# The chunk state kept in PSUM: the evacuating engines write it back, instead of identity matmuls on TensorE

## The reference

```
def step(S, inp):
    r_t, w_t, k_t, v_t, kk_t, kka_t = inp
    sa = jnp.einsum('bhvk,bhk->bhv', S, kk_t)
    S = (S * w_t[:, :, None, :]
         - sa[..., None] * kka_t[:, :, None, :]
         + v_t[..., None] * k_t[:, :, None, :])
    y_t = jnp.einsum('bhvk,bhk->bhv', S, r_t)
    return S, y_t
```

## Time and profile before

| what | us |
|---|---|
| median of 3 runs | 2519.12 (2517.28 to 2519.45) |
| the profiled execution | 2521.04 |
| its span in the trace | 2519.3 |
| TensorE busy | 2282.6 (91%) |
| VectorE busy | 1435.9 (57%) |
| ScalarE busy | 1062.2 (42%) |
| one turn of the recurrence in steady state | 38.67 |

### The profile page before, as it was taken

One profiled execution on the slowest core, in us unless ns is written; L12 is line 12 of the kernel. 1 busy time (PEld: TensorE's weight loads), 2 busy tenths in 40 slices (PEclk: granted clock), 3 DMA queues, 4 the chain that ended last, 5 costly groups with the idle time before them and its releaser, 6 DMA issues.

```text
span 2519.3 us, 43613 instructions
## 1 busy us (share of the span) xinstructions
PE 2282.6 (91%) x16514; PEld 1690.7 (67%) x16514; DVE 1435.9 (57%) x2446; ACT 1062.2 (42%) x2072; POOL 282.8 (11%) x249
## 2 busy tenths in 40 slices
PE   3789999899999999979899999988789998999998
PEld 1566776566666666658688888856666585787876
DVE  6777888344454454444555455558974565434445
ACT  3455666245455455532322222332167623323233
POOL 2101000112122121210000000019600000000000
PEclk6899999799999999969999999999999998999998
DMA  2234456313212223023233333312221031333332
GB/s 95 79 118 130 158 163 176 83 36 69 65 40 65 56 54 65 19 77 98 76 90 94 97 95 96 96 59 67 67 76 34 26 92 54 97 94 90 100 90 77
DMA packets 387985, 208.37 MB, mean 83 GB/s; under 512 B 81520, under 2 KB 370696, under 8 KB 387592
## 3 DMA queue, kind: packets, MB, share of 16 engines
q1 hardware_dynamic: 387216, 206.21, 28.9%
q10 hardware_dynamic: 632, 0.21, 0.0%
HBM read 176.96 MB, written 29.43 MB: 82 GB/s over the span
## 4 chain that ended last, share of the span: by engine, by line
PE 61%; DVE 21%; ACT 10%; issue 6%; DMA 1%; SPq 1%; DVEq 0%; POOL 0%; ACTq 0%; POOLq 0%
PE bank L1465 13%; PE bank L1467 12%; PE bank L1466 12%; PE bank L517 3%; DVE w_lo L1620 3%; DVE dconv L1873 3%; PE bank L500 2%; PE bank L482 2%; ACT w_hi L1231 2%; PE bank L539 1%; PE bank L458 1%; PE bank L504 1%; PE bank L443 1%; PE bank L432 1%; PE bank L483 1%
## 5 line engine op out<-in xcount | busy, mean ns | idle before, releaser
L1465 PE MATMUL bank<-xl,w_hi 128*128 128x512 f32 (+1 forms) x1568 | 632.7, 404 | 65.4 <-DVE xl L1625 40.0
L1466 PE MATMUL bank<-xl,w_lo 128*128 128x512 f32 (+1 forms) x1568 | 617.6, 394 | 0.0
L1467 PE MATMUL bank<-xl,w_hi 128*128 128x512 f32 (+1 forms) x1568 | 617.4, 394 | 0.0
L1231 ACT ACTIVATE w_hi<-w_raw 128x1024 fp32r<-128x1024 f32 (+2 forms) x282 | 284.7, 1010 | 421.5 <-PE bank L1467 416.8
L1620 DVE TENSOR_TENSOR w_lo<-w_raw,w_hi 128x1024 fp32r<-128x1024 f32 (+2 forms) x282 | 333.8, 1184 | 140.9 <-ACT w_hi L1231 129.4
L1465 PEld LDWEIGHTS bank<-xl,w_hi 128*128 128x128 f32 (+1 forms) x1568 | 296.6, 189 | 171.2 <-issue 48.0
L1467 PEld LDWEIGHTS bank<-xl,w_hi 128*128 128x128 f32 (+1 forms) x1568 | 297.1, 189 | 65.3 <-issue 1.8
L1466 PEld LDWEIGHTS bank<-xl,w_lo 128*128 128x128 f32 (+1 forms) x1568 | 297.6, 190 | 62.7 <-issue 4.0
L1465 PE MATMUL bank<-xh,w_hi 128*128 128x512 f32 x480 | 198.1, 413 | 51.1 <-DVE w_lo L1620 46.0
L1466 PE MATMUL bank<-xh,w_lo 128*128 128x512 f32 x480 | 192.9, 402 | 0.0
L1467 PE MATMUL bank<-xh,w_hi 128*128 128x512 f32 x480 | 192.7, 401 | 0.0
(11 more groups left out here) (321 smaller groups left out, 3645.9 us busy)
## 6 DMA issues: line engine op xcount, KB each, us to landing
w_raw<-in_a_w_in SPq DMA_DIRECT2D x64, 512.0 KB, 4.1
w_raw<-in_b_w_in SPq DMA_DIRECT2D x64, 512.0 KB, 4.0
w_raw<-in_w_ffn_up SPq DMA_DIRECT2D x44, 512.0 KB, 3.8
w_raw<-in_w_in SPq DMA_DIRECT2D x36, 512.0 KB, 3.7
w_raw<-in_a_w_out SPq DMA_DIRECT2D x16, 512.0 KB, 4.0
w_raw<-in_b_w_out SPq DMA_DIRECT2D x16, 512.0 KB, 4.0
w_raw<-in_w_ffn_down SPq DMA_DIRECT2D x16, 512.0 KB, 4.0
d_g<-sq SPq DMA_DIRECT2D x16, 256.0 KB, 2.1
```

What stands on the lines that cost most here:

```text
L1231: A(w_hi[0:rows, slot, 0:nkb, 0:ncol], w_raw[0:rows, slot, 0:nkb, 0:ncol], ACT.Copy).then_inc(s_hi, 1)
L1465: mm(outp, wh, xlo, start=start, stop=False)
L1466: mm(outp, wl, xhi, start=False, stop=False)
L1467: return mm(outp, wh, xhi, start=False, stop=stop)
```

## The change

The identity matmuls of line 449 go. In phase 2 the evacuating engine, after the copy to `sv`, executes the same operation a second time with bank 6 as its output: the scaled state stays in bank 6. The matmul of line 464 of the next chunk then adds to what stands there; for the first chunk of a tile, whose state is zero, it starts the sum. A new semaphore for each head tells TensorE that the write is done, and line 464 waits for it beside the wait for u.

```
@@ recurrence_tensor, phase 0
                     if c:
                         state_output(j, b, c)
-                    for h in range(2):
-                        mm(bank[6][rows[h], 0:C], ident[rows[h], rows[h]], sv[b][rows[h], c, h, :],
-                           start=True, stop=False)
@@ recurrence_tensor, phase 2
                         pe.wait_ge(R["u_copied"][h], NCH * j + c + 1)
+                        if c:
+                            pe.wait_ge(R["state_seeded"][h], (NCH - 1) * j + c)
                         last = mm(bank[6][rows[h], 0:C], bt[b][:, c, rows[h]], sv[b][:, c, h, :],
-                                  start=False, stop=True)
+                                  start=c == 0, stop=True, skip_group_check=True)
@@ recurrence_evac, phase 2
                 scaled(sv[b][hs, c + 1, h, :], bank[6][hs, 0:C], st_pc[j % 3][hs, c:c + 1]).then_inc(R["s_copied"][h], 1)
+                scaled(bank[6][hs, 0:C], bank[6][hs, 0:C], st_pc[j % 3][hs, c:c + 1]).then_inc(R["state_seeded"][h], 1)
```

More of the change, by code:

```diff
@@ L371, in program @@
             "centered_copied", "y_squared", "var_summed", "y_rstd_made", "y_finished", "bonus_weighted")}
-        for n in ("e_copied", "inverse_made", "state_zeroed", "tiles_loaded", "ends_loaded", "rhs_copied", "u_copied", "s_copied"):
+        for n in ("e_copied", "inverse_made", "state_zeroed", "tiles_loaded", "ends_loaded", "rhs_copied", "u_copied", "s_copied", "state_seeded"):
             R[n] = [sem(f"{n}{h}") for h in range(2)]
```

## The result

The changed kernel takes 2541.8 us (2539.8 to 2545.5, 4 runs) against 2519.3 before: 1.0086 times as long, 95% interval 1.0073 to 1.0099, 22.5 us more. The forecast of 2521.5 (2511.5 to 2530) was wrong, and its chance for "slower" was only 0.35.

The account below looks back on a forecast made before the run. TensorE was taken as the bound over most of a period; -0.36 + 0.05 + 0.20 + 0.21 + 0.05 = +0.15 us, times 15 = +2.3 us, carried to the median: 2521.5 us, range 2511.5 to 2530.

Parts of the forecast that it names:

- the sum of a period: One period of the recurrence, 38.67 us before: gains from removed matmuls and costs of added writes together +0.15 us.
- Most of the identity passes come out as nothing: Removing a chunk's two identity matmuls frees at most 0.12 us; counted as gain only at chunks 4, 6 and 7.
- steps 6 and 9: Chunks 2 and 3 of a period: TensorE waits there for VectorE anyhow, so the removed matmuls gain nothing.
- step 0: Chunk 0 of a period: the products wait until ScalarE has stored V, so the removed matmuls gain nothing.
- The near price: Cost of one added write behind an evacuation of the same partitions: 0.20 us on VectorE, 0.21 on ScalarE.
- Steps 8 and 9: VectorE's write ahead of four masks delays L787, for which TensorE waits already: +0.20 us a period.
- Step 14: ScalarE's write ahead of the weight-panel cast L655 delays the cast and TensorE's L443: +0.21 us a period.
- rival 3: Both engines swallow the writes; five chunks gain 0.12 us, less 0.10 at chunk 5: 7.5 us, 2511.6; chance 0.10.
- steps 3 and 15: Chunks 1 and 5: removed matmuls would gain, but VectorE's added writes delay TensorE's later starts: +0.05 us each.
- -0.36: Gain a period at chunks 4, 6 and 7, where TensorE's next operation starts without a wait: 3 x 0.12 us.
- The second wait costs nothing: L464's added wait on the previous chunk's write counted zero; as a rival, 0.09 us later per chunk, 2531; chance 0.07.
- the dear prices: Rival: added writes cost 0.31 us on VectorE and 0.35 on ScalarE, nothing overlapping: +9.4 us, 2528.5; chance 0.28.

## Why the prediction was wrong

The step that failed is the one by which the sum of a period was turned into time: "+0.15 us a period, times 15" took the clock as it was. The prediction had the full clock in the row of the period, named the clock only at its end as something that nothing counted, and gave it no rival and no chance. The change lengthened two waits of TensorE and took away the passes that had filled part of others. Its periods at full clock account for 1.5 of the 22.5 us; the other 21 came from the clock that this cost: 51 us at 1.2 GHz in the profiled execution.

Point by point:

- *Most of the identity passes come out as nothing*: right. The waits at steps 6 and 9 grew by the 0.12 us that each pair had filled, and at step 0 a wait of 0.35 us opened where there had been none. (The changed kernel with filler in its waits has that one too, and the full clock, so it is not enough by itself.) That this was not free was the mistake: a pass that costs no time because TensorE would wait anyhow still keeps it busy. I had written these off as "nothing".
- *The near price*, 0.20 and 0.21: right. The next operation of the same first partition starts 0.20 behind on VectorE (620.61 to 620.81) and 0.22 on ScalarE (630.91 to 631.13). PSUM as the destination costs VectorE nothing more than SBUF (275 ns both). ScalarE is faster there, 267 against the 309 ns of the evacuation. That agrees with the rule of the Trainium skill, ScalarE: Activation LUTs, Step-by-step: what each stage is for, which the prediction named.
- *Steps 8 and 9*: right, wait longer by 0.32, 0.3 forecast. *Step 14*: right, cast at 0.51, 0.54 forecast. The period grew by 0.10, +0.15 forecast. The run with passes and writes (39.14) gives the added part alone as 0.47, forecast 0.51. The run without either (38.08) gives the removed part alone as 0.59, near the 0.60 of five steps at 0.12, where rival 3 had taken 0.10 off. The two do not simply add: with the writes in place steps 3 and 15 give nothing, as the prediction said, and -0.36 + 0.47 = 0.11 is what came.
- *The second wait costs nothing*: right. In the periods looked at, no L464 (463 now) starts behind idle TensorE.
- *Rivals*: the dear prices and the second wait did not occur. The true rival was missing. The sign that could have made it one was in the view of the busy time: TensorE's clock was full in the periods before with 3 us idle in each of them, and nothing in the profile told how near that was to the edge. The trace of before does not show the edge; only a rival for it could have been set up, with a price from its other parts where the clock is halved.

The low stretches cost 18.9 us for 51 us of them, 0.37 us for each.

## What to carry to other kernels

An operation of TensorE that hides in a wait is not free to remove: it can be what holds the clock. Where a change takes matmuls away or adds to what TensorE waits for, look at the granted clock beside the idle gaps, and compare a period at full clock with one below it before looking for slower operations. If the clock is what was lost, matmuls that add zeros in the long waits can bring it back, as they did in the three filled kernels here; and here a second write of an evacuating engine cost least behind the work that others wait for (periods of 38.21 us, against 38.77 with the writes ahead of it). Look at every execution too: a good median can hide some that lost the clock.

## What the runs showed of the hardware

- TensorE's clock reacts to waits of tenths of a microsecond. In the kernel before, 0.15 us more of waiting once in a period of 38.67 us brought stretches of 6.8 us at 1.2 GHz, in two of twelve periods, 10.3 and 10.4 us behind the same instruction. The Trainium skill, TensorE: Matmul & The Clock Gate, A second HAM failure mode: psum-queue depth-cycling, tells of a kernel in which frequent short idle times between groups of matmuls made the clock swing; the runs here agree that short idle times can lower the clock, and show it for a single wait grown from 0.68 to 0.83 us. Filling that wait took it back to the time of its periods (2528.1 to 2520.7).
- Matmuls whose weights are all zero keep the clock up as well: ten pairs of them a tile, placed in the waits of the changed kernel, brought 21.6 us back (2541.8 to 2520.2).
- Not every period of a kernel loses the clock, though all have the same waits: seven of thirteen in the profiled execution of the changed kernel. Executions of one kernel then differ by up to 15 us (2512.4 to 2527.2 without passes and writes), where the kernels without excess, all but one, stay within 5 to 7. What decides which period loses it was not settled. The one is the kernel with the writes moved and filler in three waits: its wait at step 9 is 0.68 us, as before the change, and three of its ten executions had a lower granted clock; the profiled one of them lost it in the last turn. What else of a period counts, the missing passes for one, stays open.
- The share of the wait at step 15 stays open too: no kernel changed it alone. Two stretches of the changed kernel, one of that with filler at chunks 2 and 3 and two of the one with a single write moved began 22.4 to 23.0 us behind line 607, which puts them behind that wait.
